# Compression pieces of a hybrid decoder trunk in groups of four, between groups of four split pieces

## The chip, the core and the metric

The kernel runs as one program on one core of a Trainium2 chip. The metric is the device time in microseconds of that core, from the program's start to its end. All inputs come from HBM, the output goes back to HBM.

## What is computed

Two layers of a decoder trunk on 256 tokens of width 2048. In each layer one input projection feeds three token mixers (MLA, forgetting attention "fox", and sparse attention "nsa" with a compressed, a selected and a windowed branch); then an output projection and a squared-ReLU MLP. The part that matters here is the compression of the keys and values of the nsa mixer, and the projections beside it:

```python
def nsa_compress(tok, pos_emb, w1, w2):
    B, S, G, D = tok.shape
    n_cmp = (S - NSA_CMP_LEN) // NSA_CMP_STRIDE + 1
    idx = np.arange(n_cmp)[:, None] * NSA_CMP_STRIDE + np.arange(NSA_CMP_LEN)[None, :]
    blk = tok[:, idx] + pos_emb[None, None, :, None, :]
    blk = blk.transpose(0, 1, 3, 2, 4).reshape(B, n_cmp, G, NSA_CMP_LEN * D)
    return jax.nn.gelu(blk @ w1) @ w2
...
    h = rms_norm(x, norm_mix) * (1.0 + sc_a) + sh_a
    (cq, ckv, kr, fq, fk, fv, ff,
     nq, nkc, nvc, nks, nvs, nkw, nvw, ng) = jnp.split(h @ w_in, split_points, axis=-1)
    ...
    k_cmp = nsa_compress(kc, pos_k, ck_w1, ck_w2)
    v_cmp = nsa_compress(vc.reshape(kv_shape), pos_v, cv_w1, cv_w2)
```

The first weight of each compression, `w1`, has 4096 x 512 elements, for only 30 rows of blocks (padded to 32).

## The kernel before

**Pieces.** All weights are streamed through SBUF in pieces of 256 rows x up to 512 columns (512 KB). The list `ORDER` gives the order of the 158 pieces of a layer ahead of its MLP (FRONT); `PIECES` is the whole program. A *split piece* is an ordinary projection piece: ScalarE writes its rounded high half `w_hi` (line 774), VectorE the remainder `w_lo` (L1256), and TensorE makes twelve matmuls of it (`product`, L1740 to L1742: two row blocks, two token halves, three terms). A *compression piece*, `cw1`, isn't split: TensorE multiplies it as it landed, in full float32, with a stationary block of 128 x 32 (`compress`, L1764). Four such matmuls go to four groups of 32 columns of the array; in the trace each is two passes, so two pieces are eight. There are 32 compression pieces in each layer, 16 for the keys (`w_raw<-in_nsa_cmp_k_w`) and 16 for the values.

**Groups.** Line 53, `CLUSTER = 2`: the loop behind it goes over the positions of the compression pieces in `ORDER` and, for every `CLUSTER` of them, moves them behind the split pieces between the first and the last of these positions. So two compression pieces stand together, usually between two and two split pieces. `compress` waits at the first of a group for all of the group to have landed, so that their matmuls run as one burst. Work of TensorE that hangs on a position inside a group (`PE_POST`: transposes "T", attention slots, the sums of the forget gates) is moved behind the group's last piece by `CLUSTER_LAST`.

**Ring.** `w_raw` has 7 slots (`RAW`) which split pieces, compression pieces and tiles of the adaLN weights (ada tiles, two layers' modulation; VectorE, L1183) share in the order in which VectorE comes to them. The SyncE queue issues loads in that order (L662, L681); each waits for the slot of the item seven places before: for `lo_done` of a split piece, `ada_used` of a tile, `piece_used` (TensorE) of a compression piece. `w_hi` and `w_lo` have 4 slots, so ScalarE and VectorE run at most four split pieces ahead of TensorE.

**Side work.** Steps of ScalarE and VectorE hang on positions too (`SIDE`), by position number, not by piece: evacuations of accumulators, softmax of attention slots, ada tiles. Ada tiles are spread over the positions that aren't compression pieces. On both engines a position's own split comes first, then its side steps. The chunks that the text speaks of: `vs` and `vw` (nsa values), `kv0`, `kv1` (MLA), `nqa`, `nqb` (nsa queries). `vs`, `vw`, `nqa` and `nqb` all use accumulator 0; each may begin only when the one before has been copied out. The copy of vw is L1335 and L1336, that of nqa L1327 and L1328 on VectorE. Attention slot s (`slot`) makes the values of unit s-2, the scores of unit s (L1787, L1788 or L1791) and the transposed probabilities of unit s-1 (L1799); its scores wait for the exponentials of the unit before (L925, L927 on ScalarE). An ada block ends with a transpose and a sum (L1194).

Of the kernel before, what the change touches and what calls it, by code (L numbers as in the profile page):

```python
# [49 lines left out]
ORDER += ["wo2"] * 2 + ["wo3"] * 8  # L50


CLUSTER = 2
CLUSTER_LAST = {}
at_cw1 = [q for q, name in enumerate(ORDER) if name == "cw1"]
for i in range(0, len(at_cw1), CLUSTER):
    q0, q1 = at_cw1[i], at_cw1[i + CLUSTER - 1]
    ORDER[q0:q1 + 1] = [name for name in ORDER[q0:q1 + 1] if name != "cw1"] + ["cw1"] * CLUSTER
    CLUSTER_LAST.update({q: q1 for q in range(q1 + 1 - CLUSTER, q1 + 1)})
FRONT = len(ORDER)  # L60
assert FRONT == 158 and ORDER.count("cw1") == 32, FRONT

# [113 lines left out]
for l in range(LAYERS):  # L176
# [5 lines left out]
    if l == 0:  # L182
# [4 lines left out]
        for b in range(1, 4):  # L187
            q = 6 * b
# [124 lines left out]
    for s in range(SUPERS):  # L313
        for j in range(4):
            q = M + 64 * s + 8 * (4 + j) + 10
# [133 lines left out]
def trunk(nc, x, c, positions, inv_freq, ada_w, ada_b, norm_mix, norm_mlp, w_in, fox_b_f, mla_q_norm, mla_w_uq,  # L449
          mla_kv_norm, mla_w_ukv, nsa_pos_k, nsa_pos_v, cmp_k_w1, cmp_k_w2, cmp_v_w1, cmp_v_w2,  # L450
          out_norm, w_out, mlp_w1, mlp_w2, final_norm, out):
    with ExitStack() as ctx:
# [126 lines left out]
        def t_is_free(l, name):  # L579
            return t_free[T_BANK[l, name]], T_NO[l, name] + 1  # L580
# [994 lines left out]
        def _(pe):  # L1575
# [172 lines left out]
            def compress(Q):  # L1748

                l, chunk, p = PIECES[Q]  # L1750
                j = p // 16
                if p == 0:
                    pe.wait_ge(acc_free[1], ACC_USE[l, chunk])
                if p % 16 == 0:
                    pe.wait_ge(*t_is_free(l, ("kcT", "vcT")[j]))
                if p % CLUSTER == 0:
                    for piece in range(Q, Q + CLUSTER):
                        n = RING_NO["lo", piece]
                        pe.wait_ge(raw_landed[n % RAW], 16 * (n // RAW + 1))
                i = RING_NO["lo", Q]  # L1760
                for k in range(2):
                    kt = (p % 16) * 2 + k
                    part = 32 * (kt % 4)
                    mm = pe.matmul(acc[1][part:part + 32, j, :], blk[j][:, kt, :], w_raw[:, i % RAW, k, :],  # L1764
                                   start=kt < 4, stop=kt >= 28)
                mm.then_inc(piece_used, 1)
# [66 lines left out]
            for Q in range(ALL):  # L1833
                if Q + 4 in BORDERS:
                    for q in range(Q, Q + 4):
                        product(q, (0,))
                if Q in BORDERS:
                    for q in range(Q, Q + 3):
                        product(q, (0,))
                    for kind, l, what in PE_PRE[Q]:  # L1840
                        t_in(l, what)
                    product(Q + 3, (0,))
                elif Q == 0:
                    for kind, l, what in PE_PRE[Q]:
                        t_in(l, what)
                if any(B - 4 <= Q < B + 4 for B in BORDERS):
                    product(Q, (1,))
                elif PIECES[Q][1] == "cw1":
                    compress(Q)
                else:  # L1850
                    product(Q)
                then(Q)
# [25 lines left out]
```

## Time and profile before

| | us |
|---|---|
| median of 3 runs | 2435.87 |
| lowest, highest | 2433.2, 2439.37 |
| the profiled execution | 2436.38 |
| its span (first to last instruction) | 2434.5 |
| TensorE busy | 2327.7 (96%) |
| TensorE's weight loads busy | 1912.0 (79%) |
| VectorE busy | 1718.7 (71%) |
| ScalarE busy | 1139.3 (47%) |
| mean granted TensorE clock | 0.989 |

Of the chain of work that ended last 82% is TensorE, 7% VectorE, 5% DMA. A total of 633.90 MB goes through the DMA queues, at a mean of 260 GB/s. The compression pieces lie between 188.8 and 306.2 us in layer 0 and between 1379.8 and 1486.9 us in layer 1. TensorE's busy share is modelled from pipelined matmuls: consecutive starts tell how fast it goes, the wait in square brackets behind a row tells the idle time before it and what ended it.

### The profile page before, as it was taken

To read this page: it belongs to the slowest core of one execution; us is meant where nothing else is said; L and a number is where in the kernel's file an instruction comes from. 1 tells how busy PE (TensorE), PEld (TensorE's weight loads), DVE (VectorE), ACT (ScalarE), POOL (GpSimd) and SP (SyncE) were. 2 spreads that over 40 slices of the span, in tenths; PEclk is the share of its full clock that TensorE was granted. 3 is DMA by queue.
4 is the path that set the end of the run, shared out by engine and by line. 5 is a ranking of instruction groups with operands and counts; after the bars stand their busy time and mean duration, and the time that the engine had idled before them with its cause. 6 is when DMAs were issued, how large, how long until landed. Compare 5 with 4: busy or idle time off the path is not lost.

```text
span 2434.5 us, 29301 instructions
## 1 busy us (share of the span) xinstructions
PE 2327.7 (96%) x11145; PEld 1912.0 (79%) x11145; DVE 1718.7 (71%) x2094; ACT 1139.3 (47%) x1584; POOL 19.2 (1%) x52
## 2 busy tenths in 40 slices
PE   3798999999999999999999999999999999999998
PEld 2686778778888888888878777888788888888887
DVE  7985788889787787887767667786666555555455
ACT  3253355545534434434446445454553453443453
POOL 1000000000000000000000000000000000000000
PEclk9799999999999999999999999999999999999999
DMA  9979986889889899898878798466677666666653
GB/s 367 384 257 337 332 283 204 270 295 329 286 303 313 298 329 321 299 327 300 299 239 273 252 319 279 152 217 208 211 258 239 183 188 196 185 189 191 190 186 126
DMA packets 318611, 633.90 MB, mean 260 GB/s; under 512 B 20428, under 2 KB 41352, under 8 KB 317832
## 3 DMA queue, kind: packets, MB, share of 16 engines
q1 hardware_dynamic: 314432, 625.49, 76.8%
q10 hardware_dynamic: 4040, 6.54, 0.8%
q8 instruction: 89, 1.46, 0.2%
q14 instruction: 50, 0.41, 0.1%
HBM read 629.85 MB, written 2.10 MB: 260 GB/s over the span
## 4 chain that ended last, share of the span: by engine, by line
PE 82%; DVE 7%; DMA 5%; ACT 2%; issue 2%; SPq 1%; POOL 0%; ACTq 0%; POOLq 0%; DVEq 0%
PE acc L1740 18%; PE acc L1742 17%; PE acc L1741 17%; PE pair L1740 7%; PE pair L1742 7%; PE pair L1741 7%; DVE ada_acc L1183 3%; DMA w_raw<-in_w_in 2%; DMA arena<-in_ada_w 2%; DVE w_lo L1256 2%; PE bank_T L1600 1%; PE acc L1764 1%; PE pair L1791 1%; PE bank_O L1600 1%; ACT w_hi L774 1%
## 5 line engine op out<-in xcount | busy, mean ns | idle before, releaser
L1256 DVE TENSOR_TENSOR w_lo<-w_raw,w_hi 128x1024 fp32r<-128x1024 f32 (+3 forms) x764 | 906.4, 1190 | 399.0 <-ACT w_hi L774 397.6
L774 ACT ACTIVATE w_hi<-w_raw 128x1024 fp32r<-128x1024 f32 (+3 forms) x764 | 785.4, 1031 | 755.2 <-PE acc L1742 437.1
L1740 PE MATMUL acc<-w_hi,hT_hi 128*128 128x512 f32 (+3 forms) x1536 | 611.6, 398 | 28.9 <-DVE w_lo L1256 12.4
L1742 PE MATMUL acc<-w_lo,hT_hi 128*128 128x512 f32 (+3 forms) x1536 | 590.6, 385 | 0.0
L1741 PE MATMUL acc<-w_hi,hT_lo 128*128 128x512 f32 (+3 forms) x1536 | 590.0, 384 | 0.0
L1183 DVE SCALAR_TENSOR_TENSOR ada_acc<-w_raw,silu_c,ada_acc 128x1024 f32<-128x1024 f32 x300 | 383.5, 1278 | 1.1 <-DVE small L1336 0.4
L1740 PEld LDWEIGHTS acc<-w_hi,hT_hi 128*128 128x128 f32 x1536 | 292.1, 190 | 101.2 <-DVE w_lo L1256 21.9
L1742 PEld LDWEIGHTS acc<-w_lo,hT_hi 128*128 128x128 f32 x1536 | 291.9, 190 | 56.3
L1741 PEld LDWEIGHTS acc<-w_hi,hT_lo 128*128 128x128 f32 x1536 | 292.7, 191 | 51.2 <-issue 1.7
L1740 PE MATMUL acc<-w_hi,uT_hi 128*128 128x512 f32 (+1 forms) x656 | 257.0, 392 | 0.0
L1742 PE MATMUL acc<-w_lo,uT_hi 128*128 128x512 f32 (+1 forms) x656 | 254.7, 388 | 0.0
L1741 PE MATMUL acc<-w_hi,uT_lo 128*128 128x512 f32 (+1 forms) x656 | 254.5, 388 | 0.0
L1740 PE MATMUL pair<-w_hi,hT_hi 128*128 128x512 f32 (+1 forms) x448 | 179.3, 400 | 17.9 <-DVE w_lo L1256 17.9
L1742 PE MATMUL pair<-w_lo,hT_hi 128*128 128x512 f32 (+1 forms) x448 | 173.3, 387 | 0.0
L1741 PE MATMUL pair<-w_hi,hT_lo 128*128 128x512 f32 (+1 forms) x448 | 173.0, 386 | 0.0
L1740 PE MATMUL pair<-w_hi,uT_hi 128*128 128x512 f32 (+1 forms) x416 | 163.3, 393 | 0.9 <-DVE w_lo L1256 0.9
L1742 PE MATMUL pair<-w_lo,uT_hi 128*128 128x512 f32 (+1 forms) x416 | 161.2, 388 | 0.0
L1741 PE MATMUL pair<-w_hi,uT_lo 128*128 128x512 f32 (+1 forms) x416 | 161.1, 387 | 0.0
L1742 PEld LDWEIGHTS acc<-w_lo,uT_hi 128*128 128x128 f32 x656 | 123.1, 188 | 25.2
L1740 PEld LDWEIGHTS acc<-w_hi,uT_hi 128*128 128x128 f32 x656 | 123.2, 188 | 25.0 <-issue 0.5
L1741 PEld LDWEIGHTS acc<-w_hi,uT_lo 128*128 128x128 f32 x656 | 123.2, 188 | 24.9 <-issue 0.5
L1740 PEld LDWEIGHTS pair<-w_hi,hT_hi 128*128 128x128 f32 x448 | 85.5, 191 | 37.0 <-DVE w_lo L1256 19.8
(256 smaller groups left out, 1927.2 us busy)
## 6 DMA issues: line engine op xcount, KB each, us to landing
w_raw<-in_mlp_w SPq DMA_DIRECT2D x512, 512.0 KB, 4.8
w_raw<-in_ada_w SPq DMA_DIRECT2D x320, 512.0 KB, 5.7
w_raw<-in_w_in SPq DMA_DIRECT2D x112, 512.0 KB, 5.3
arena<-in_ada_w SPq DMA_DIRECT2D x64, 512.0 KB, 11.2
w_raw<-in_w_out SPq DMA_DIRECT2D x64, 512.0 KB, 5.6
w_raw<-in_nsa_cmp_k_w SPq DMA_DIRECT2D x32, 512.0 KB, 6.7
w_raw<-in_nsa_cmp_v_w SPq DMA_DIRECT2D x32, 512.0 KB, 6.4
w_raw<-in_w_in SPq DMA_DIRECT2D x16, 388.0 KB, 5.3
```

The source lines that it names most:

```text
L774: a.activation(w_hi[:, at % RING, :, 0:n], w_raw[:, i % RAW, :, 0:n], ACT.Copy).then_inc(hi_done, 1)
L1183: ins = v.scalar_tensor_tensor(ada_acc[:], raw, silu_c[:, kt:kt + 1], ada_acc[:], ALU.mult, ALU.add)
L1256: v.tensor_tensor(w_lo[:, at % RING, :, 0:n], w_raw[:, RING_NO["lo", Q] % RAW, :, 0:n], w_hi[:, at % RING, :, 0:n].bitcast(F32), ALU.subtr ...
L1600: mm = pe.transpose(bank[:, k, P * m:P * m + P], halves[m], ident[:])
L1740: pe.matmul(o, st_hi[:, kt + k, tok], wh, start=first and k == 0, stop=False)
L1741: pe.matmul(o, st_lo[:, kt + k, tok], wh, start=False, stop=False)
L1742: mm = pe.matmul(o, st_hi[:, kt + k, tok], wl, start=False, stop=last and k == 1)
L1764: mm = pe.matmul(acc[1][part:part + 32, j, :], blk[j][:, kt, :], w_raw[:, i % RAW, k, :], start=kt < 4, stop=kt >= 28)
L1791: mm = pe.matmul(o, NQ[:, h, qt], k_[:, h // 4, 0:keys], start=True, stop=True)
```

## The change

Four compression pieces stand together instead of two, so four split pieces stand between two groups where there were two. The matmuls still run in bursts of two pieces (`BURST`): `compress` waits at every second piece for it and the next to have landed, and the work of TensorE that hangs inside a group is moved behind the burst that it falls into, not behind the group. Nothing else is edited. Lines behind the edit stand one further down.

```diff
-CLUSTER = 2
+CLUSTER, BURST = 4, 2
 CLUSTER_LAST = {}
 at_cw1 = [q for q, name in enumerate(ORDER) if name == "cw1"]
 for i in range(0, len(at_cw1), CLUSTER):
     q0, q1 = at_cw1[i], at_cw1[i + CLUSTER - 1]
     ORDER[q0:q1 + 1] = [name for name in ORDER[q0:q1 + 1] if name != "cw1"] + ["cw1"] * CLUSTER
-    CLUSTER_LAST.update({q: q1 for q in range(q1 + 1 - CLUSTER, q1 + 1)})
+    for q in range(q1 + 1 - CLUSTER, q1 + 1, BURST):
+        CLUSTER_LAST[q] = q + BURST - 1
...
-                if p % CLUSTER == 0:
-                    for piece in range(Q, Q + CLUSTER):
+                if p % BURST == 0:
+                    for piece in range(Q, Q + BURST):
```

On VectorE at the hand-over of accumulator 0 from vw to nqa in layer 0, before (L1498 to L1515 are attention slots, L1256 the split of an nqa piece, L1335 and L1336 the copy of vw, L1183 an ada tile):

```order
194 L1498 RECIPROCAL small<-small 128x2
195 L1507 TENSOR_SCALAR arena<-bank_O,small 128x128 x2
196 L1513 TENSOR_TENSOR pair<-pair,causal 128x2x128
197 L1514 TENSOR_REDUCE small<-pair 128x1
198 L1515 TENSOR_REDUCE small<-pair 128x1
199 L1256 TENSOR_TENSOR w_lo<-w_raw,w_hi 128x2x388
200 L1335 COPY arena<-acc 128x512
201 L1336 COPY small<-acc 128x48
```

The same place in the changed kernel:

```order
194 L1184 SCALAR_TENSOR_TENSOR ada_acc<-w_raw,silu_c,ada_acc 128x1024
195 L1257 TENSOR_TENSOR w_lo<-w_raw,w_hi 128x2x388
196 L1499 RECIPROCAL small<-small 128x2
197 L1508 TENSOR_SCALAR arena<-bank_O,small 128x128 x2
198 L1514 TENSOR_TENSOR pair<-pair,causal 128x2x128
199 L1515 TENSOR_REDUCE small<-pair 128x1
200 L1516 TENSOR_REDUCE small<-pair 128x1
201 L1184 SCALAR_TENSOR_TENSOR ada_acc<-w_raw,silu_c,ada_acc 128x1024
202 L1336 COPY arena<-acc 128x512
203 L1337 COPY small<-acc 128x48
```

The split now stands ahead of the slot's work, and an ada tile directly ahead of the copy of vw. On TensorE two compression pieces and a slot stood between the last vw product and the first nqa product; now nothing stands there.

On VectorE at the hand-over from nqa to nqb in layer 0, before (L1498 to L1504 slot 7, L1216 and L1489 the norm of the MLA output, L1256 the split of the first nqb piece, L1194 an ada sum, L1327 and L1328 the copy of nqa):

```order
244 L1498 RECIPROCAL small<-small 128x2
245 L1500 TENSOR_TENSOR small<-small 128x2
246 L1504 SCALAR_TENSOR_TENSOR arena<-bank_O,small,arena 128x128 x2
247 L1216 TENSOR_SCALAR small<-small 128x2
248 L1489 TENSOR_SCALAR arena<-arena,small 128x4x128 x2
249 L1256 TENSOR_TENSOR w_lo<-w_raw,w_hi 128x1024
250 L1194 TENSOR_REDUCE small<-bank_T 128x4
251 L1327 COPY ybuf<-acc 128x2x384
252 L1328 TENSOR_TENSOR small<-acc,fbias 128x8
```

The same place in the changed kernel:

```order
243 L1257 TENSOR_TENSOR w_lo<-w_raw,w_hi 128x1024
244 L1499 RECIPROCAL small<-small 128x2
245 L1501 TENSOR_TENSOR small<-small 128x2
246 L1505 SCALAR_TENSOR_TENSOR arena<-bank_O,small,arena 128x128 x2
247 L1217 TENSOR_SCALAR small<-small 128x2
248 L1490 TENSOR_SCALAR arena<-arena,small 128x4x128 x2
249 L1195 TENSOR_REDUCE small<-bank_T 128x4
250 L1328 COPY ybuf<-acc 128x2x384
251 L1329 TENSOR_TENSOR small<-acc,fbias 128x8
```

The split of the first nqb piece moved from behind slot 7 and the norm to ahead of them. On TensorE the pair that stood between the last nqa and the first nqb is gone.

On TensorE at attention slot 9 of layer 0, before (L1740 to L1742 the end of an nqb product, L1661 to L1663 the sums of the forget gates, L1764 a burst of two compression pieces, L1791 the scores of slot 9; those of slot 8 are rows 891 and 892, one whole product further up):

```order
902 L1740 MATMUL acc<-w_hi,hT_hi 128x512
903 L1741 MATMUL acc<-w_hi,hT_lo 128x512
904 L1742 MATMUL acc<-w_lo,hT_hi 128x512
905 L1661 MATMUL bank_T<-arena,small 8x128
906 L1662 MATMUL bank_T<-ones,small 8x128
907 L1663 MATMUL bank_T<-arena,small 8x128
908 L1764 MATMUL acc<-w_raw,arena 32x512 x4
909 L1791 MATMUL pair<-arena 128x128
910 L1791 MATMUL pair<-arena 128x256
911 L1799 MATMUL pair<-ident,arena 128x128 x3
```

The same place in the changed kernel:

```order
901 L1765 MATMUL acc<-w_raw,arena 32x512 x4
902 L1792 MATMUL pair<-arena 128x128
903 L1792 MATMUL pair<-arena 128x256
904 L1662 MATMUL bank_T<-arena,small 8x128
905 L1663 MATMUL bank_T<-ones,small 8x128
906 L1664 MATMUL bank_T<-arena,small 8x128
907 L1765 MATMUL acc<-w_raw,arena 32x512 x4
908 L1792 MATMUL pair<-arena 128x128
909 L1792 MATMUL pair<-arena 128x256
910 L1800 MATMUL pair<-ident,arena 128x128 x3
```

The scores of slot 8 (902, 903) now stand between the two bursts of a group, and no product lies between them and the scores of slot 9 (908, 909).

## Rows read from the trace of the kernel before

**Rows 1.** Windows: span, busy us of each engine (instructions), clock, DMA share, GB/s
```profile
182.00:310.00 128.00, 112.48 (x660) 85.20 (x659) 84.33 (x149) 49.65 (x94) 1.29 (x3) 0.97 0.94 337
1380.00:1490.00 110.00, 104.90 (x624) 79.09 (x617) 66.30 (x120) 47.61 (x91) 1.29 (x3) 0.98 0.91 316
...
310.00:320.00 10.00, 10.00 (x46) 8.30 (x45) 9.83 (x17) 6.68 (x16) 0.00 (x0) 0.83 1.03 388
```

**Rows 2.** TensorE's waits, 182 to 310 us: total us, times, longest
```profile
PE acc L1740 <- DVE w_lo L1256: 5.8, 7, 1.7
PE acc L1740 <- DVE small L1328: 3.5, 1, 3.5
PE pair L1791 <- ACT arena L927: 2.7, 1, 2.7
PE pair L1787 <- ACT arena L927: 1.7, 1, 1.7
```

**Rows 3.** TensorE's waits, 1380 to 1490 us
```profile
PE acc L1740 <- DVE small L1328: 3.1, 1, 3.1
```

**Rows 4.** The SyncE queue's waits, in 182:310 and in 1380:1490
```profile
SPq L662 <- PE acc L1764: 56.4, 15, 8.3
...
SPq L662 <- PE acc L1764: 74.0, 16, 9.7
```

**Rows 5.** Timeline of TensorE, layer 0: start, us, instruction
```profile
202.55 0.39 PE L1742 MATMUL acc<-w_lo,hT_hi 128*128 128x512 f32 x1
202.87 1.07 PE L1764 MATMUL acc<-w_raw,arena 128*32 128x512 f32 x8
```

**Rows 6.** Timeline at the hand-over from vw to nqa, layer 1
```profile
1431.68 1.06 PE L1764 MATMUL acc<-w_raw,arena 128*32 128x512 f32 x8
...
1432.34 0.68 DVE L1335 COPY arena<-acc 128x512 f32<-128x512 f32 x1
...
1432.68 0.49 PE L1811 MATMUL bank_O<-arena 128*128 128x128 f32 x2
1432.94 0.20 DVE L1336 COPY small<-acc 128x48 f32<-128x48 f32 x1
...
1435.01 0.42 PE L1740 MATMUL acc<-w_hi,hT_hi 128*128 128x388 f32 x1
```

**Rows 7.** Timelines at slots 8 and 9, layer 1
```profile
1482.29 0.81 PE L1791 MATMUL pair<-arena 128*128 128x128 f32 x4
...
1485.78 0.38 PE L1661 MATMUL bank_T<-arena,small 128*8 128x128 f32 x2
...
1486.23 0.63 PE L1764 MATMUL acc<-w_raw,arena 128*32 128x512 f32 x3
...
1486.53 0.20 ACT L927 ACTIVATION_READ_ACCUMULATOR arena<-pair,small 128x1 f32 x1
```

**Rows 8.** Timelines at slots 8 and 9, layer 0, the brackets are idle time before
```profile
299.21 0.47 SPq L662 DMA_DIRECT2D w_raw<-in_w_in  x1
...
306.22 1.06 ACT L774 ACTIVATE w_hi<-w_raw 128x1024 fp32r<-128x1024 f32 x1 [5.71 <-DMA w_raw<-in_w_in]
...
311.27 0.63 PE L1741 MATMUL acc<-w_hi,hT_lo 128*128 128x512 f32 x1
311.70 0.63 PE L1742 MATMUL acc<-w_lo,hT_hi 128*128 128x512 f32 x1
```

**Rows 9.** Timelines at the hand-over from nqa to nqb, layer 1
```profile
1459.55 1.04 SPq L662 DMA_DIRECT2D w_raw<-in_w_in  x1
...
1459.63 0.16 DVE L1498 RECIPROCAL small<-small 128x2 f32<-128x2 f32 x1
...
1461.51 0.92 DVE L1489 TENSOR_SCALAR arena<-arena,small 128x512 f32<-128x512 f32 x2 [0.81 <-POOL small L739]
1463.22 1.06 ACT L774 ACTIVATE w_hi<-w_raw 128x1024 fp32r<-128x1024 f32 x1 [3.14 <-DMA w_raw<-in_w_in]
```

## The prediction

> **What bounds the kernel now.** I read the windows first. In the stretch where layer 0 runs its compression pieces (182 to 310 us) TensorE is busy 112.48 of 128 us and the DMA share is 0.94; in layer 1 (1380 to 1490) it is 104.90 of 110 us and 0.91 [rows 1]. So layer 0 runs close to what its loads allow, and layer 1 is bound by TensorE with loads close behind. The change touches nothing outside these two stretches and their edges. Then I read what TensorE waits for. In layer 0: 5.8 us in seven waits for the low halves (w_lo), 3.5 us for L1328, 2.7 and 1.7 us for exponentials (L927) [rows 2]. In layer 1 the one long wait is again L1328, 3.1 us [rows 3]. L1328 is the last read of the accumulator of nqa: nqb uses the same bank and can't start before it. Third, the SyncE queue stood still for compression matmuls for 56.4 us in layer 0 and 74.0 us in layer 1 [rows 4]: it loads in ring order, and a slot that holds a compression piece is free only when TensorE has used it, where VectorE frees the slot of a split piece up to four pieces ahead.
>
> A long idle time also costs clock. Behind the 2.7 us wait matmuls of 512 columns started 0.43 us apart (311.27 and 311.70) and took 0.63 us, where one at the granted clock of 1.00 took 0.39 [rows 5, 8]; the window around them has a mean clock of 0.83 [rows 1]. That is the 1.2 GHz level, and at that spacing a product of twelve matmuls takes twice its 2.7 us. The 1.7 us waits did not show it.
>
> **The change part by part.** No matmul, transfer or split is added or removed. What moves is which pieces stand next to each other, and what stands between them.
>
> *Edges.* A pair of compression pieces (eight passes) begins 0.09 us after the product before it is through (202.55 plus a spacing of 0.23, against 202.87) [rows 5], and the next step begins 1.00 us after the pair's start (1431.68, 1432.68) [rows 6]. Two pairs behind one another could save the 0.09 and at most a quarter of the 1.00, if a column group of the second pair starts when that of the first is free: 0.34 at most, 0.2 taken. But transposes and attention steps still stand between most of the pairs. Only one group of layer 0 and two of layer 1 have nothing between their halves: 3 x 0.2 = 0.6 us saved. Bounds: nothing, and 16 x 0.34 = 5.4 us. The Trainium skill (TensorEngine Tiling, Tiling Modes, Key Properties) says that a change of tiling mode drains TensorE, which speaks for fewer groups; with the transposes between the halves the number of mode changes hardly falls, and by the full rule the saving would be that upper bound.
>
> *vw to nqa.* Both chunks use accumulator 0. Before, a compression pair and an attention slot stand between the last vw and the first nqa: from 1431.68 to 1435.01, 3.3 us of cover. VectorE begins to copy vw out at 1432.34 and is through at 1432.94 + 0.20 = 1433.14, 1.5 us after the last vw product [rows 6]. Now the first nqa stands right behind the last vw, so in layer 1 that time is bare: about 0.1 us for the release makes 1.6 us. In layer 0 it is worse. VectorE reaches this copy only behind the ada tile that stands ahead of it in its order, and by the ring the slot of that tile is one freed by the fourth compression piece of the group just done. A load issued with others in flight took 7.0 us to be used (issue 299.21, ScalarE 306.22) [rows 8]; with 6 for this one, a tile of 1.28 and a copy of 1.1 us the copy ends 8.4 us after that group. TensorE has a slot (1432.68 to 1435.01 is 2.3, and 0.2 for its wait) and one vw product (12 matmuls of 280 columns at 0.23 x 280/512, 1.5) until then: 4.4 us idle, and, as behind the 2.7 us wait, slow products for 1.3 us. Bounds for layer 0: 1.6 (load already there) and 7.
>
> *nqa to nqb.* The first nqb now follows the last nqa, without the pair (1.00) between. Before, this wait is that for the load: issue 1459.55, ScalarE at 1463.22, and VectorE through with slot 7 and the MLA norm long before (1461.51 + 0.92) [rows 9]. Now that load hangs on an earlier piece of compression and comes in time in layer 1, but the slot's and norm's VectorE work (1459.63 to 1462.43, 2.8 us) stands behind the split, directly ahead of the copy. I get 2.1 us of wait for 3.1: 1.0 saved in layer 1. In layer 0 one more ada load and the ada sum stand in front: from the use of the piece that frees the slot, 7.2 (load) + 2.3 (split) + 3.0 + 0.7 + 1.1 = 14.3 us, against 8.7 us of TensorE work (an estimate from the same rows: slot 6 and the kcmp step 1 each, a pair 1.0, slot 7 0.9, two nqa products of 12 x 0.23 x 388/512 = 2.1, a transpose step 0.6): 5.6 for 3.5, 2.1 lost. Bounds: -3.5 to +3 in each layer.
>
> *Attention slots that move together.* Slot s may only compute its scores when the exponentials of slot s-1 are there. Slots 8 and 9 now have only the forget gates' sum (1485.78 to 1486.23, 0.45) and one pair (1.00) between them, no longer a nqb product. In layer 1 the scores of slot 8 end at 1482.29 + 0.81 = 1483.10 and their exponentials at 1486.53 + 0.20 = 1486.73, 3.6 us [rows 7]. 3.6 - 1.45 = 2.2 us of new wait in layer 1. In layer 0 there already are 2.7 us at this place [rows 2], behind a late load (ScalarE waited 5.71 us for it) [rows 8] which now is issued earlier: 0. Slots 1 and 2, with a pair between: 0.4 each layer. Slot 1 of layer 0 waited 1.7 us for L927 behind a late split [rows 2]; it now stands behind a pair whose loads come after that split, so this goes: -1.7. Bounds of all this: -3 to +6.
>
> *The ring.* Four held slots of seven leave three to load ahead. In layer 1 the third vw of a group hangs on the first piece of the group before. A load there took 3.7 us [rows 9], plus some 1.5 of split, against 5.5 us of TensorE work (a pair, two vw products, a transpose step, the scores of slot 0): nearly hidden. I take 0.6 us in all, bounds 0 and 12 (below).
>
> *Sum.* Layer 1: -0.4 + 1.6 - 1.0 + 2.2 + 0.4 + 0.6 = +3.4. Layer 0: -0.2 + 4.4 + 1.3 + 2.1 + 0.4 - 1.7 = +6.3. Layer 0 gives part of it back: its loads are the limit, TensorE's later waits for them (w_lo, L1328, L927 in rows 2) shorten when it comes later. The loads were idle only 0.06 x 128 = 7.7 us, and a stop of TensorE costs only where the loads stop too. I take back 4: +2.3. Together +5.7 us. The profiled execution took 2436.38 us (span 2434.5), 0.5 above the median of the runs, 2435.87. So 2442 us.
>
> **The rivals.** A measurement of this kernel can tell about 0.3%, 7.3 us, from no change; so faster means under 2428.6, slower over 2443.2.
>
> (a) *The forecast's mechanism*, +1 to +12 us with my sizes, 50%; a little under half of that lies beyond 2443.2.
>
> (b) *The ring starves, slower.* In every group SyncE waits until TensorE has taken the first of four pieces, and the loads restart from empty. For it: SyncE's longest stop for compression is already 8.3 and 9.7 us [rows 4] with two held slots. Against it: the DMA share of 0.94 and 0.91 in spite of that [rows 1]. It decides from where three loads ahead last less long than four split products. Price: about 1 us more at each of 16 groups less what is counted, +12 to +18: 2450. 20%.
>
> (c) *Loads decide alone, no change.* Every new wait falls into time in which TensorE would have waited for a load anyway; in layer 0 that is the whole 5.8 + 3.5 + 2.7 + 1.7, and in layer 1 copies are quicker than I think. Then only the edges and 2 us of waits remain: 2435 to 2438. Against it: layer 1 has little such idle time [rows 3]. 20%.
>
> (d) *Fewer long idles, faster.* The three waits of 3.5, 3.1 and 2.7 us all bring slow products behind them. If the regrouping turns each into one of 1.7 or less, 4.2 us of waiting and some 5 us of slow clock go, and the edges bring 1 to 5: 2426. Against it: VectorE's order ahead of both copies gets longer, not shorter. 10%. By the edges' rule of the Trainium skill (the same page and section) alone, 5.4 us would go from the two edge terms, which doesn't reach 0.3% either.
>
> **How the numbers follow.** The likeliest case is (a), 2442 us. Half of (a) less a little, 27%, and (c), 20%, are within 0.3%: 47%. Slower: 23% of (a) and the 20% of (b): 43%. Faster: (d), 10%. For the range I leave out the lower end of (d) and the upper end of (b): 2432 to 2453.
>
> **What would show it.** Right: in the profile of the changed kernel a new wait of the first nqa for L1337 (the last read of vw, one line further down), about 1.6 us in layer 1 and longer in layer 0; a wait for the exponentials (L928) in layer 1 between 2 and 3 us at slot 9; a shorter wait for L1329 in layer 1 and a longer one in layer 0; the DMA share of layer 0 slightly under 0.94 over the same pieces. The starving ring would show as many waits for w_lo, over 15 us in all, and a DMA share well under 0.9. The loads-decide case would show the new waits, but w_lo waits gone in return and the last compression pair at the same time. Wrong altogether would be a difference that lies outside the two stretches: the MLP should keep its length within 1 us.

## The result, and the profile of the changed kernel

The changed kernel takes 2453.13 us (median of 4 runs, 2451.14 to 2456.71), against 2436.65 us for the kernel before in 4 runs: a ratio of 1.0069, with a 95% interval of 1.0056 to 1.0082. That is 16.5 us or 0.7% slower. The prediction said 2442, which counts as no change, with a range up to 2453: the outcome that it thought likeliest did not come, and the time lies just beyond the end of the range. The profiled execution of the changed kernel took 2454.85 us, with a span of 2453.0 (18.5 more than the one before).

The busy times hardly moved. The page of the changed kernel:

```profile
span 2453.0 us, 29302 instructions
...
PE 2331.0 (95%) x11145; PEld 1914.6 (78%) x11145; DVE 1717.6 (70%) x2094; ACT 1139.4 (46%) x1584; POOL 19.3 (1%) x52
```

So the time is idle time and slow clock, not work. To find its place I cut both traces at the starts of the same products, so that a stretch holds the same products in both. The windows of layer 0, of the kernel before and then of the changed kernel (columns as in [rows 1]); the first stretch goes from the fifth vw product to the third nqa product, the second on to the second nqb product, the third on to the first product of the next chunk:

```profile
229.00:257.40 28.40, 25.09 (x170) 19.70 (x170) 19.66 (x34) 12.29 (x30) 0.00 (x0) 1.00 1.03 380
257.40:291.30 33.90, 29.14 (x168) 23.47 (x168) 26.21 (x60) 12.37 (x26) 1.29 (x3) 0.90 0.88 313
291.30:323.70 32.40, 29.63 (x153) 22.94 (x150) 24.39 (x36) 15.30 (x27) 0.00 (x0) 0.95 0.98 356
...
230.50:268.10 37.60, 28.73 (x170) 22.71 (x170) 19.87 (x34) 12.27 (x30) 0.00 (x0) 0.86 0.78 284
268.10:303.60 35.50, 29.29 (x169) 23.08 (x169) 27.43 (x61) 12.30 (x26) 1.28 (x3) 0.90 0.85 299
303.60:336.00 32.40, 28.32 (x152) 21.58 (x149) 23.57 (x33) 15.40 (x27) 0.00 (x0) 1.00 1.00 368
```

The same three stretches of layer 1:

```profile
1417.20:1442.10 24.90, 24.77 (x171) 19.65 (x171) 15.26 (x31) 10.60 (x28) 0.00 (x0) 1.00 0.97 334
1442.10:1472.10 30.00, 26.93 (x164) 21.58 (x161) 22.26 (x53) 12.71 (x26) 1.29 (x3) 0.94 0.85 296
1472.10:1499.90 27.80, 27.80 (x153) 21.70 (x150) 19.08 (x31) 15.19 (x27) 0.00 (x0) 1.00 0.94 340
...
1431.10:1460.40 29.30, 26.10 (x173) 21.18 (x171) 14.18 (x30) 10.48 (x29) 0.00 (x0) 0.94 0.75 272
1460.40:1488.00 27.60, 25.17 (x161) 20.58 (x161) 22.67 (x55) 12.24 (x26) 1.28 (x3) 1.00 0.86 304
1488.00:1518.50 30.50, 28.46 (x154) 21.66 (x150) 19.77 (x31) 15.30 (x27) 0.00 (x0) 1.00 0.99 355
```

The second column is the length. Layer 0: +9.2, +1.6 and 0.0 us, and +1.5 ahead of the first stretch (0.3 of it before the first compression piece, the rest a wait of 1.74 us at a transpose with matmuls at 1.2 GHz behind it). Layer 1: +4.4, -2.4 and +2.7. Together 17.0 of the 18.5 us; the rest, 1.6, comes later in layer 0, at 450 us, and is told under the hardware. Half of everything is one stretch of 37.6 us: the hand-over from vw to nqa in layer 0. Its clock is 0.86 where it was 1.00.

What TensorE waits for there (the stretch 230.5 to 268.1 us, then 268.1 to 303.6 us of layer 0, then 1431.1 to 1460.4 us of layer 1; total us, times, longest):

```profile
PE acc L1741 <- DVE small L1337: 5.7, 1, 5.7
PE acc L1765 <- DMA w_raw<-in_nsa_cmp_k_w: 2.5, 1, 2.5
PE acc L1741 <- DVE w_lo L1257: 1.6, 3, 1.0
...
PE acc L1741 <- DVE small L1329: 3.7, 1, 3.7
...
PE acc L1741 <- DVE small L1337: 2.8, 1, 2.8
```

L1337 is the last read of the accumulator of vw. That wait is new. In [rows 2, 3] nothing answers to it.

What VectorE did ahead of this copy in layer 0 is the timeline of that engine (start, length, instruction, in brackets the idle time before and what ended it), with two rows of TensorE around it:

```profile
239.78 1.94 PE L1765 MATMUL acc<-w_raw,arena 128*32 128x512 f32 x8 [2.53 <-DMA w_raw<-in_nsa_cmp_k_w]
...
243.80 0.43 DVE L1514 TENSOR_TENSOR pair<-pair,causal 128x256 f32<-128x256 f32 x1 [6.05 <-PE pair L1789]
...
245.87 2.67 DVE L1184 SCALAR_TENSOR_TENSOR ada_acc<-w_raw,silu_c,ada_acc 128x1024 f32<-128x1024 f32 x2
...
253.12 1.27 DVE L1184 SCALAR_TENSOR_TENSOR ada_acc<-w_raw,silu_c,ada_acc 128x1024 f32<-128x1024 f32 x1
254.31 0.68 DVE L1336 COPY arena<-acc 128x512 f32<-128x512 f32 x1
254.91 0.20 DVE L1337 COPY small<-acc 128x48 f32<-128x48 f32 x1
...
255.16 0.69 PE L1741 MATMUL acc<-w_hi,hT_hi 128*128 128x388 f32 x1 [5.68 <-DVE small L1337]
255.64 0.53 PE L1742 MATMUL acc<-w_hi,hT_lo 128*128 128x388 f32 x1
...
260.22 0.34 PE L1742 MATMUL acc<-w_hi,hT_lo 128*128 128x388 f32 x1
```

Read from the top: TensorE waits 2.53 us for a compression piece and then runs that burst at half speed (1.94 us where [rows 5] has 1.07). The scores of the slot behind it come late by that much, and VectorE, which can't pass them, stands still for 6.05 us. From 243.80 on it is dense: slot 1, the last split of vw and two of nqa with three ada tiles between them, the work of slot 2, one more ada tile, and only then the copy of vw. From the scores of slot 1 on VectorE has 11.3 us of work up to the end of this copy (255.11), TensorE only 5.7 us up to the end of vw (about 249.5). That difference is the wait. The 6.05 us ahead of it put both engines back alike and don't lengthen it: in experiment 2 VectorE stands 1.12 us at this place and the wait is 5.6 us, in experiment 4 it stands 5.72 us and the wait is 0.9. Behind the wait nqa matmuls of 388 columns take 0.53 us, and at 260.22 again the 0.34 of the full clock: between them lies a stretch at 1.2 GHz.

### The profile page after: what moved, and what is told of

It reads as the page before. It is cut to its first block, busy times and chain, and to the rows that moved or that the text cites. A ratio compares the mean times of both kernels' runs of the same rounds, so it can differ in the third digit from the quotient of the medians.

```text
span 2453.0 us, 29302 instructions
## 1 busy us (share of the span) xinstructions
PE 2331.0 (95%) x11145; PEld 1914.6 (78%) x11145; DVE 1717.6 (70%) x2094; ACT 1139.4 (46%) x1584; POOL 19.3 (1%) x52
## 4 chain that ended last, share of the span: by engine, by line
PE 80%; DVE 8%; DMA 6%; ACT 2%; issue 2%; SPq 1%; POOL 0%; ACTq 0%; POOLq 0%; DVEq 0%
PE acc L1741 17%; PE acc L1743 17%; PE acc L1742 17%; PE pair L1741 7%; PE pair L1743 7%; PE pair L1742 7%; DVE ada_acc L1184 3%; DMA arena<-in_ada_w 3%; DMA w_raw<-in_w_in 2%; DVE w_lo L1257 2%; PE bank_T L1601 1%; PE bank_O L1601 1%; ACT w_hi L775 1%; PE pair L1792 1%; PE acc L1765 1%
## 5 line engine op out<-in xcount | busy, mean ns | idle before, releaser
L1742 PE MATMUL acc<-w_hi,hT_lo 128*128 128x512 f32 (+3 forms) x1536 | 589.7, 384 | 0.0
L1742 PEld LDWEIGHTS acc<-w_hi,hT_lo 128*128 128x128 f32 x1536 | 293.1, 191 | 51.2 <-issue 1.7
L1742 PE MATMUL acc<-w_hi,uT_lo 128*128 128x512 f32 (+1 forms) x656 | 254.5, 388 | 0.0
L1742 PE MATMUL pair<-w_hi,hT_lo 128*128 128x512 f32 (+1 forms) x448 | 173.0, 386 | 0.0
L1742 PE MATMUL pair<-w_hi,uT_lo 128*128 128x512 f32 (+1 forms) x416 | 161.7, 389 | 0.0
L1742 PEld LDWEIGHTS acc<-w_hi,uT_lo 128*128 128x128 f32 x656 | 123.2, 188 | 25.0 <-issue 0.5
## 6 DMA issues: line engine op xcount, KB each, us to landing
arena<-in_ada_w SPq DMA_DIRECT2D x64, 512.0 KB, 11.3
```

The lines of the kernel that those rows point to most:

```text
L1742: pe.matmul(o, st_lo[:, kt + k, tok], wh, start=False, stop=False)
```

## The experiments

My theory (H) was that the loss sits at the hand-overs of accumulator 0, because VectorE reaches the copies too late. The rival (R) was the ring: with four slots held by compression pieces too few loads run ahead. The kernel before took 2435.82 us in the runs beside experiments 1 to 4, and 2435.02 beside 5 to 8.

**1 and 2. Groups of four in one half only.** The first 16 compression pieces of each layer in fours and the rest in twos, and the other way round. In the first, both hand-overs stand as in the kernel before; in the second, both as in the changed kernel.

```diff
-CLUSTER = 2
+GROUPS, BURST = [4] * 4 + [2] * 8, 2     # 2: [2] * 8 + [4] * 4
...
-for i in range(0, len(at_cw1), CLUSTER):
+for size in GROUPS:
```

> Groups of four only for the first 16 compression pieces of each layer (keys), groups of two for the other 16 (values), bursts of two everywhere. Theory H (hand-over): what costs is that the last vw and the first nqa product stand side by side, so that the copy of accumulator 0 is bare, and that nqb follows nqa; both places then look as before, and the kernel takes 2436 to 2440 us. Theory R (ring): what costs is that four held slots leave three to load ahead; half of the groups are of four, so half of the 16.5 us stay: 2443 to 2446.

Measured for the first half: 2438.26 us, a ratio of 1.0010 (1.0001 to 1.0019).

> The mirror: groups of two for the first 16 compression pieces of each layer, groups of four for the other 16. Theory H: nqa to nqb and attention slot 9 as in the change; the hand-over from vw to nqa again has a group between the two chunks or not, by the positions; if the wait for the copy of vw is there, 2447 to 2453 us, and if it is gone, 2438 to 2442. Theory R: 2443 to 2446 whether that wait is there or not.

Measured for the second half: 2451.18 us, 1.0064 (1.0049 to 1.0079). The two losses, 2.4 and 15.4 us, add up to 17.8, about the 16.5 of the whole change. (In the single traces they don't: by the starts of products the two lose 8.0 us of layer 0 together, where the changed kernel loses 12.0.) TensorE's long waits in layer 0 (182 to 320 us) in the first-half kernel (L1331 is the last read of nqa), and then in the second-half kernel (L1339 of vw):

```profile
PE acc L1743 <- DVE small L1331: 2.5, 1, 2.5
...
PE acc L1743 <- DVE small L1339: 5.6, 1, 5.6
...
PE acc L1743 <- DVE small L1331: 3.7, 1, 3.7
```

The 5.6 us wait for vw comes with the second half and with it alone. If the ring starved in every group of four, half of the groups would have cost half. They cost a seventh.

**3. Copy of vw two positions earlier, in the changed kernel.** Only VectorE's order changes: the copy stands ahead of slot 2's work and of the last ada tile.

```diff
-                    (56, "kv1"), (72, "vw"), (89, "nqa"), ...
+                    (56, "kv1"), (70, "vw"), (89, "nqa"), ...
```

> The changed kernel with one side step moved: the copy of vw out of accumulator 0 hangs on position 70 instead of 72, so VectorE makes it right behind the split of the first nqa piece, ahead of one more split, attention slot 2 and two ada tiles. Theory H: the wait of 5.7 us in layer 0 falls to about 1, that of 2.8 in layer 1 to about 1.2, and the slow products behind them (1.9 and 1.5 us) go: 2443 to 2446 us. Theory R: TensorE then waits for split pieces that aren't loaded, and the time stays at 2450 to 2453.

Measured: 2445.89 us, 1.0043 (1.0028 to 1.0058), 7.2 us less than the changed kernel (6.4 if each is set against the kernel before in the runs beside it). The wait for L1337, in layer 0 and in layer 1, and a wait for a compression load in layer 1:

```profile
PE acc L1741 <- DVE small L1337: 1.3, 1, 1.3
...
PE acc L1741 <- DVE small L1337: 0.9, 1, 0.9
PE acc L1765 <- DMA w_raw<-in_nsa_cmp_k_w: 2.1, 1, 2.1
```

No load was moved. So the 5.7 us were VectorE's order and not a load that came late for it. By the starts of products, counted from the product at 178 us, ahead of the first compression piece, layer 0 loses 1.5 us where the changed kernel loses 12.0. Layer 1 gains nothing in this trace (4.9 lost, for 4.6): the 2.1 us wait for a load (at 1428.98), which the changed kernel has with 0.5 us and experiment 4 hasn't at all, stands in for the one for the copy. That is R at work, in one trace of three with the same order of pieces.

**4. Both copies early.** The copy of nqa too, from position 89 to 86 and first there.

```diff
-                    (56, "kv1"), (72, "vw"), (89, "nqa"), ...
-        side(F + q, ("evac", l, name), 4 if name in ("kc", "uq1") else 0)
+                    (56, "kv1"), (70, "vw"), (86, "nqa"), ...
+        side(F + q, ("evac", l, name), 4 if name in ("kc", "uq1") else -1 if name == "nqa" else 0)
```

> As the run with the early copy of vw, and also the copy of nqa right behind the split of the first nqb piece (position 86), ahead of attention slot 7, the MLA norm and the ada sum. Theory H: 2 to 4 us less than with the vw copy alone, 2440 to 2443 us: the waits for L1329 of 3.7 and 2.4 us fall to about 1.3 each. Theory R: no difference to the other over 1 us.

Measured: 2438.01 us, 1.0006 (0.9996 to 1.0016): no difference from the kernel before that can be told, and 15.1 us less than the changed kernel (14.3 against the kernels before beside them). The order of the pieces is that of the changed kernel throughout. By the starts of products in the two traces, the first product behind the compression stretch of layer 0 begins 0.04 us earlier than in the kernel before, where it was 12.3 later in the changed kernel. The waits for nqa's copy (L1329), layer 0 and layer 1:

```profile
PE acc L1741 <- DVE small L1329: 0.7, 1, 0.7
...
PE acc L1741 <- DVE small L1329: 1.1, 1, 1.1
```

This came out better than I expected, by 2 us: the slow products behind both waits went too. Not all of it takes back what the change cost. The first stretch of layer 0 still loses 2.5 us, with a wait of 2.0 for a compression load; the second and third are 2.1 and 2.0 us shorter than in the kernel before, whose own wait of 3.5 us for the copy of nqa is down to 0.7 here. In layer 1 3.0 us are lost between the fifth and the seventh nqb product, at slots 8 and 9, and 3.3 gained ahead of them. The 2.4 us by which the trace is longer than that of the kernel before come from neither layer's compression stretch but from the place at 450 us (2.7).

**5 and 6. Half of each compression load, in fours and in twos.** Each compression piece loads only 128 of its 256 rows; TensorE's work is the same. This gives the ring time.

```diff
+                if chunk == "cw1":
+                    sp.dma_start(w_raw[:, at, 0, 0:n], src[0:P, :]).then_inc(raw_landed[at], 16)
+                else:
```

> The changed kernel, but each compression piece loads only its first 128 of 256 rows (256 KB for 512 KB); TensorE still multiplies both halves, so half of the compression weights is left out of the result. 16 MB less go through the two stretches. To be set against the same edit of the kernel before. Theory H (VectorE's order at the two hand-overs): the difference between fours and twos stays at 9 us or more, and the waits for L1337 and L1329 stay over 2 us in layer 1. Theory R (the ring starves the loads): the difference falls under 5 us.

Measured, in fours: 2444.36 us, 1.0043 of the kernel before (1.0029 to 1.0056).

> The kernel before with the same half loads of the compression pieces (half of their weights is left out). Both theories: a little faster than before, since layer 0 is close to its loads: 2422 to 2432 us. The number that decides is the difference to the run with groups of four and half loads.

Measured, in twos: 2425.79 us, 0.9956 (0.9941 to 0.9971). With half of the loads the fours are slower than the twos by 18.6 us, no less than with all of them. The windows 182 to 320 and 1385 to 1510 us of the fours (the DMA share is the last but one number), and the wait for vw (L1340) in layer 0:

```profile
182.00:320.00 138.00, 117.07 (x683) 88.93 (x682) 87.99 (x154) 51.59 (x101) 1.29 (x3) 0.96 0.77 259
1385.00:1510.00 125.00, 117.13 (x705) 90.47 (x703) 77.23 (x150) 54.91 (x108) 1.29 (x3) 1.00 0.76 258
...
PE acc L1744 <- DVE small L1340: 6.7, 1, 6.7
```

A DMA share of 0.77 and 0.76, where the changed kernel has 0.85 in both windows, lets the wait stand, even longer. R falls as the main cause. A part of it lives on. The 2.5 us wait for a compression load is down to 0.2, and the fours' loss in layer 0, by the starts of products, is 9.3 us with half loads and 12.3 with full ones. But 2.0 of these 3.0 us lay between the traces at 178 us already, ahead of the first compression piece; counted from there the loss is 11.1 for 12.0, and in layer 1 it is 6.6 for 4.6. On the other side the first stretch of layer 0 loses 6.6 us in experiment 2, which has no wait for such a load, for 9.2. So the ring's part of layer 0 is 1 to 3 us, and these single traces don't tell it more closely.

**7. Copy of nqa early, in the kernel before.** If late copies cost the kernel before as well, this should make it faster.

```diff
-                    (56, "kv1"), (72, "vw"), (89, "nqa"), ...
+                    (56, "kv1"), (72, "vw"), (86, "nqa"), ...   # and first there, as in 4
```

> The kernel before with one side step moved: the copy of nqa directly behind the split at position 85, ahead of attention slot 7 and the MLA norm, instead of behind the split of the first nqb piece. The waits for L1328 (3.5 and 3.1 us) end when the first nqb piece is split, 1.0 to 1.6 us earlier, and with less slow clock behind them: 2431 to 2435 us. If the copy isn't what holds nqb there, no change.

Measured: 2442.49 us, 1.0031 (1.0020 to 1.0043), slower where I expected faster. VectorE's timeline in layer 1:

```profile
1458.54 0.97 DVE L1256 TENSOR_TENSOR w_lo<-w_raw,w_hi 128x776 fp32r<-128x776 f32 x1 [0.64 <-ACT w_hi L774]
1462.62 0.96 DVE L1327 COPY ybuf<-acc 128x768 f32<-128x768 f32 x1 [3.11 <-PE acc L1742]
```

TensorE's waits there:

```profile
PE acc L1740 <- DVE w_lo L1256: 6.7, 3, 5.5
```

VectorE now stands at the copy for 3.11 us until the last nqa product is through, and the work of slot 7, the norm and the split of the first nqb piece wait behind it. TensorE's wait for the copy is gone, and a wait of 5.5 us for that split has taken its place. The same edit that gains 7.9 us in the changed kernel (experiment 4 against 3) loses 7.5 here: with a pair of compression pieces between nqa and nqb the cover is on the copy's side, without it the copy is what TensorE needs next. The Trainium skill (TensorE: Matmul & The Clock Gate, Architectural detail) has VectorE's queue as strictly first in, first out; the 3.11 us, with a split standing behind the copy, agree.

**8. As 4, with the scores of slot 8 one position earlier.** To take the two slots apart that 4 still pays for.

```diff
-SLOT_AT = [...] + [95, 97, 99, ...
+SLOT_AT = [...] + [94, 97, 99, ...
```

> The changed kernel with both copies early, and attention slot 8 behind position 94 instead of 96: ahead of the last group, so that its softmax has both bursts to run beside. If the 2.4 us that are left with both copies early in layer 1 come from slots 8 and 9 standing one burst apart, 1.0 to 2.5 us go: 2435 to 2437 us. If they come from the ring, none.

Measured: 2441.23 us, 1.0023 (1.0013 to 1.0034): 6.2 us over the kernel before, where 4 was 2.2 over it. By the starts of products the loss between the fifth and the seventh nqb product of layer 1 is 3.8 us (2.96 to 6.79), where 4 has 3.0 (-0.58 to +2.42). It is 0.8 us more than in 4 at the same place of layer 0 too. So the move didn't open the gap that it was meant to open, and I didn't find an order that beats the kernel before. Of the 4.0 us between the two medians these places hold 1.6; the rest, and why the move costs at all, stays open.

## Why the prediction was wrong, step by step

**The mechanism was mostly the right one, at the places named.** It promised a new wait for L1337 longer in layer 0 than in layer 1 (5.7 and 2.8), a wait for L1329 shorter in layer 1 (2.4 us for 3.1) and longer in layer 0 (3.7 for 3.5), and a later slot 9. The MLP kept its length. Two signs did not come: the wait for exponentials at slot 9 was 0.52 us and not 2 to 3, and the DMA share over layer 0's pieces (182 to 326 us) was 0.86, not slightly under 0.94. What failed is size: the term vw to nqa in both layers, and the 4 us that layer 0 was to give back.

**The give-back of 4 us in layer 0 failed whole.** The prediction took layer 0's losses to +6.3 and then back to +2.3, since its loads are the limit. Layer 0 lost 12.3 (12.0 from 178 us on). The waits for a split did shorten, from 5.8 us to 2.5 in all, but the waits of transposes for a copy grew by more (L1600 and L1647, now L1601 and L1648: from 1.4 us to 5.8), and the loads didn't go on. The changed kernel while TensorE stood at the hand-over, and right behind:

```profile
249.50:255.20 5.70, 0.04 (x1) 0.04 (x1) 5.54 (x11) 1.61 (x7) 0.00 (x0) 0.81 1.03 387
255.20:265.10 9.90, 9.90 (x53) 8.93 (x57) 1.83 (x6) 0.90 (x3) 0.00 (x0) 0.76 0.29 112
```

During the stop the loads ran on, at a share of 1.03. Then the free slots were used up, and for 9.9 us the share was 0.29: SyncE stood for the burst at 264.03, which the stop had put back. So the share of the first stretch fell from 1.03 to 0.78. I had written that a stop of TensorE costs only where the loads stop too, and didn't ask whether they would. They do, a little later, since a compression slot is freed by TensorE itself. And the premise was too strong: experiment 6 halves the compression loads of the kernel before and gains 9.2 us in all, by the products' starts 6.5 us in layer 0 from 178 us on and 6.0 in layer 1. The layer with a DMA share of 0.94 [rows 1] gained hardly more than the one with 0.91, which I had called bound by TensorE.

**vw to nqa was mis-sized in both layers, and is the step that failed most: +6.4 us predicted, slots 1 and 2 included, +13.6 measured.** In layer 0 I had 4.4 us of wait and 1.3 of clock; with slots 1 and 2 (+0.4 and -1.7) that makes +4.4 for the first stretch. It was +9.2: waits of 9.8 us (5.7, 2.5, 1.6) in place of 3.5, and the rest slow clock: about 2.2 in the nqa products from 255.16 on (fifteen matmuls, 0.33 us apart on average where full clock has 0.175) and 0.9 in the burst at 239.78. My sum for VectorE asked when the one ada tile ahead of the copy would have its load. It left out that the copy hangs on a position number and so stands behind everything VectorE has for that position: two slots' work and four tiles. Experiments 3 and 4 show it: the wait falls to 1.3 and 0.9 us without a load moved. The 2.5 us wait for a load ahead of it, for which the prediction had nothing in layer 0, is the ring. In layer 1 the wait was 2.8, not 1.6, because slot 2's work is ahead of the copy, and I had forgotten to price the clock there: TensorE's products behind it are slow too. Predicted +2.0 with slots 1 and 2, measured +4.4. The timeline of the changed kernel in layer 1:

```profile
1445.63 0.16 DVE L1499 RECIPROCAL small<-small 128x2 f32<-128x2 f32 x1
...
1447.35 0.68 DVE L1336 COPY arena<-acc 128x512 f32<-128x512 f32 x1
...
1448.19 0.69 PE L1741 MATMUL acc<-w_hi,hT_hi 128*128 128x388 f32 x1 [2.79 <-DVE small L1337]
...
1449.33 0.53 PE L1741 MATMUL acc<-w_hi,hT_hi 128*128 128x388 f32 x1
```

In the kernel before the copy began 0.66 us after the burst behind the last vw product did [rows 6]; here 1.95 us pass between the end of vw (1445.40) and the copy, and the slot's VectorE work from 1445.63 on fills them.

**nqa to nqb came out near in length, in layer 0 by luck.** Layer 0: +2.1 predicted, +1.6 measured. But the wait for the copy was to grow from 3.5 us to 5.6 and grew to 3.7; the rest of the 1.6 us is other waits, 1.0 us for exponentials (L1800) among them. Layer 1: -1.0 predicted, -2.4 measured; the wait is shorter by 0.7 and the slow products behind it (clock 0.94 before) are gone, which again was a clock term left out. Experiments 4 and 7 show how much this place decides in either direction.

**Slots 8 and 9 came out right in sum, for another reason.** +2.2 predicted in layer 1, +2.7 measured; nothing in layer 0, as predicted. But of the 2.2 us at slot 9 only 0.52 is there:

```profile
1495.22 0.44 PE L1601 MATMUL bank_T<-ident,ybuf 128*128 128x128 f32 x2 [1.00 <-ACT arena L830]
...
1502.08 0.92 PE L1792 MATMUL pair<-arena 128*128 128x128 f32 x4
...
1505.12 0.92 PE L1792 MATMUL pair<-arena 128*128 128x128 f32 x4 [0.52 <-ACT arena L928]
```

The exponentials now follow the scores by 2.1 us (1503.0 to 1505.07), not by 3.6: before, a split of ScalarE (1.06 us) and the load of its table for the exponentials (1.28 us) stood between, and now both lie ahead of or beside the scores. The same 0.5 comes again at slot 10 (at 1510.31), and 1.0 us at a transpose that waits for ScalarE's copy of the one before. The total agrees by luck.

**The ring.** 0.6 us in all were predicted, with bounds of 0 and 12. The experiments put 1 to 3 us on it in layer 0; in layer 1 the changed kernel's trace shows 0.5 us of wait for a load. The rival "ring starves", at 2450, was near the time and wrong in cause: SyncE's stops for compression fell in sum instead of growing, though the longest grew (10.4 and 11.2 us for 8.3 and 9.7). Its waits in 182 to 320 us and 1385 to 1500 us of the changed kernel, against 56.4 and 74.0 in [rows 4]:

```profile
SPq L663 <- PE acc L1765: 28.0, 9, 6.3
SPq L682 <- PE acc L1765: 26.2, 4, 10.4
...
SPq L663 <- PE acc L1765: 43.0, 10, 11.2
```

**Edges.** One group has its two bursts back to back in layer 0 (264.03: sixteen passes, the next step at 265.88). 1.85 us against twice 1.00, and one 0.09 less in front: 0.24, where 0.2 was taken. The rule of the Trainium skill (TensorEngine Tiling, Tiling Modes, Key Properties), that a change of mode drains TensorE, would have given the upper bound; on this row a pair joined to another saves a quarter of a microsecond, how much of it a drain is not told by any run, and the number of such changes hardly fell.

**The total.** Predicted +5.7, medians +16.5, traces +18.5. Of the 12.8 us between sum and traces, 4 are the give-back, 4.8 and 2.4 the first stretch of layers 0 and 1, and 1.6 a slow stretch further down that isn't the change's. These make 12.8; the terms left over, up and down, cancel within 0.1.

## What to carry to other kernels

When work is moved so that two users of one accumulator stand next to each other, read what the copying engine has in its queue ahead of the copy, all of it, and set it against what TensorE has left to do from the same point on; the difference is the wait, and the side work's position numbers have to move with the pieces. A high DMA share doesn't promise that a new stall will be absorbed: ask who frees the buffers, and if it is the stalled engine, give nothing back. Price the clock as a risk at every new wait, in each layer, not only at the longest: here it fell behind waits of 1.7, 2.5, 2.8 and 5.7 us and did not behind others of 2.4 and 3.4.

## What the runs showed of the hardware

**The same wait does not always cost clock.** At about 450 us, in the output projection that the change doesn't touch, TensorE waits 3.4 us for exponentials in every trace. The kernel before, and the changed kernel:

```profile
442.05 0.49 PE L1784 MATMUL pair<-arena 128*128 128x128 f32 x2 [3.38 <-ACT arena L927]
...
454.39 0.79 PE L1785 MATMUL pair<-arena 128*128 128x128 f32 x2 [3.40 <-ACT arena L928]
```

The windows of the four microseconds from there (the granted clock is the third number from the end):

```profile
442.00:446.00 4.00, 3.95 (x21) 3.44 (x22) 1.83 (x5) 3.37 (x8) 0.00 (x0) 1.00 0.67 211
...
454.30:458.30 4.00, 3.90 (x14) 3.35 (x15) 1.82 (x5) 1.70 (x5) 0.00 (x0) 0.57 0.74 257
```

In the kernel before the clock stays at 1.00 for the next 12 us. In all nine other traces it falls to 1.2 GHz for 3 to 6 us: at once, as here, or about a microsecond after the wait. By the starts of products this is 1.6 to 2.7 us between the traces in which nothing else differs there. So a difference of this size between two single traces, at a wait that the edit didn't touch, says nothing on the edit, and the medians (+16.5) are the better measure than the profiled spans (+18.5). What decides it, these runs don't tell. The Trainium skill (TensorE: Matmul & The Clock Gate, What's actually happening) lets the point of such a transition vary with where the first matmul happens to lie; the differing starts of the slow stretch agree.

**Shorter idle times than I had counted on cost clock as well, but not always.** Behind 2.53 us (239.78) and 2.79 us (1448.19) of waiting the matmuls were at 1.2 GHz; the prediction priced the clock only once, behind the longest wait. In the changed kernel it happened behind 1.74 us too, where the 1.7 us waits of the kernel before had not shown it:

```profile
214.69 0.66 PE L1648 MATMUL bank_T<-ident,ada_acc 128*128 128x128 f32 x4 [1.74 <-ACT arena L830]
...
217.40 0.63 PE L1742 MATMUL pair<-w_hi,uT_lo 128*128 128x512 f32 x1
```

And behind the 2.4 us wait for L1329 in layer 1 the clock stayed at 1.00 (the window 1460.40 to 1488.00 above).
